# The RWKV-7 block's chunk inverses: 16 by 16 blocks by forward substitution on VectorE, then two doubling levels in place of five

## The reference, cut to what matters

```python
def wkv7_scan(r, decay, k, v, a_vec, b_vec):
    def step(s, inp):
        r_t, w_t, k_t, v_t, a_t, b_t = inp
        sa = jnp.einsum('bhvk,bhk->bhv', s, a_t)
        s = (s * w_t[:, :, None, :] + sa[..., None] * b_t[:, :, None, :]
             + v_t[..., None] * k_t[:, :, None, :])
        y = jnp.einsum('bhvk,bhk->bhv', s, r_t)
        return s, y
```

## Time and profile before

| | |
|---|---|
| median of 3 runs | 2805.22 us (2804.65 to 2805.6) |
| span of the profiled execution | 2808.4 us |
| TensorE busy, matmul / weight load | 2701.1 us (96%) / 2321.6 us (83%) |
| VectorE, ScalarE, GpSimd busy | 1584.7, 1051.3, 638.2 us |
| the chunk stage, from its first instruction to its barrier | 212.4 to 293.6 us |

### The profile page before, as it was taken

How to read it: one execution, slowest core, us unless ns; L and a number is a source line. 1 busy time by engine, 2 the same in 40 slices (tenths; PEclk the granted TensorE clock), 3 DMA queues, 4 the chain that set the end, 5 groups by cost and what they waited for, 6 DMA issues and landing times. The chain is left out here.

```text
span 2808.4 us, 42550 instructions
## 1 busy us (share of the span) xinstructions
PE 2701.1 (96%) x16610; PEld 2321.6 (83%) x16610; DVE 1584.7 (56%) x2463; ACT 1051.3 (37%) x1827; POOL 638.2 (23%) x518
## 2 busy tenths in 40 slices
PE   8999999999999999998999999999999999999998
PEld 6779877788888777877888888986888899999987
DVE  5976557466653456865533336975544446666643
ACT  4364333442222333354423224546443243322223
POOL 3430101221100113442100003346444320211101
PEclk9999899999999999999999999999899999999999
DMA  4200231122222322211322222210111132222221
GB/s 163 92 9 8 90 102 64 38 90 98 98 98 98 118 75 68 92 49 64 93 97 97 98 98 76 88 64 2 52 35 40 34 121 91 83 93 93 94 98 60
DMA packets 64276, 219.08 MB, mean 78 GB/s; under 512 B 8182, under 2 KB 8822, under 8 KB 63830
## 3 DMA queue, kind: packets, MB, share of 16 engines
q1 hardware_dynamic: 61190, 211.62, 22.6%
q10 hardware_dynamic: 2896, 4.82, 0.5%
HBM read 210.07 MB, written 6.32 MB: 77 GB/s over the span
## 5 line engine op out<-in xcount | busy, mean ns | idle before, releaser
L308 PE MATMUL ps<-normed,slab_parts 128*128 128x512 f32 (+3 forms) x2280 | 789.1, 346 | 24.8 <-DVE normed L650 11.2
L310 PE MATMUL ps<-normed,slab_parts 128*128 128x512 f32 (+3 forms) x2280 | 767.0, 336 | 0.0
L309 PE MATMUL ps<-normed,slab_parts 128*128 128x512 f32 (+3 forms) x2280 | 766.6, 336 | 0.0
L163 ACT ACTIVATE slab_parts<-ring 128x1024 fp32r<-128x1024 f32 x360 | 380.3, 1057 | 897.4 <-PE ps L310 879.9
L167 DVE TENSOR_TENSOR slab_parts<-ring,slab_parts 128x1024 fp32r<-128x1024 f32 x345 | 461.5, 1340 | 377.5 <-ACT slab_parts L163 374.6
L308 PEld LDWEIGHTS ps<-normed,slab_parts 128*128 128x128 f32 x2280 | 432.6, 190 | 79.6 <-issue 20.0
L309 PEld LDWEIGHTS ps<-normed,slab_parts 128*128 128x128 f32 x2280 | 432.7, 190 | 47.6 <-issue 5.3
L310 PEld LDWEIGHTS ps<-normed,slab_parts 128*128 128x128 f32 x2280 | 432.0, 189 | 44.5
L308 PE MATMUL ps<-hidden,slab_parts 128*128 128x512 f32 x560 | 219.2, 391 | 5.6 <-DVE hidden L258 5.6
L309 PE MATMUL ps<-hidden,slab_parts 128*128 128x512 f32 x560 | 219.0, 391 | 0.0
L310 PE MATMUL ps<-hidden,slab_parts 128*128 128x512 f32 x560 | 219.0, 391 | 0.0
(11 more groups left out here) (607 smaller groups left out, 4331.1 us busy)
## 6 DMA issues: line engine op xcount, KB each, us to landing
ring<-in_stream SPq DMA_DIRECT2D x376, 512.0 KB, 3.3
scratch_gates<-fox_y SPq DMA_DIRECT2D x12, 258.0 KB, 2.2
branch_gates<-scratch_gates ACTq DMA_DIRECT2D x1, 2064.0 KB, 15.1
h<-in_x SPq DMA_DIRECT2D x8, 256.0 KB, 6.2
scratch_fox_y<-fox_y SPq DMA_DIRECT2D x1, 1032.0 KB, 6.3
gdn_z<-scratch_gates ACTq DMA_DIRECT2D x1, 1032.0 KB, 4.9
fox_y<-scratch_fox_y ACTq DMA_DIRECT2D x1, 1032.0 KB, 17.2
mix_y<-in_sgu_b SPq DMA_DIRECT2D x1, 1024.0 KB, 6.5
```

The source lines that it names most:

```text
L163: self.nc.scalar.activation(self.hi[:, n % PARTS, :], self.ring[:, n % SLOTS, :], ACT.Copy).then_inc(self.hi_ready, 1)
L308: nc.tensor.matmul(to, lhsT[0], rhs[0], start=start, stop=False)
L309: nc.tensor.matmul(to, lhsT[0], rhs[1], start=False, stop=False)
L310: return nc.tensor.matmul(to, lhsT[1], rhs[0], start=False, stop=stop)
```

## The change

- The first part has four groups of products, not five: a by b, k by a, b by r, k by r. The group whose result was the transposed first level is gone.
- `LowerBlocks` is new. After VectorE has drained `amat` and `akT`, it turns the eight diagonal 32 by 32 squares of the 16 matrices (4 instructions, `take`), so that each of 128 partitions holds one 16 by 16 diagonal block; two instructions pick the right half. `solve` does forward substitution on all 128 blocks at once: 15 steps of a multiplication and an addition, each waiting for the one before. `place` writes the inverses back: two instructions and 4 transposes, into `invT`.
- Only the last two levels are left on TensorE (`LV = 2`), with the product by `amask` ahead of the transpose.
- The k by r result is copied out by ScalarE and masked by GpSimd; `amask` is made by GpSimd too. VectorE drains the b by r result after the inverses are placed.
- TensorE runs ten products of constants between the value products and the first level (`warm(K, 2, 10)`).
- The order of the block copies on ScalarE is b, a, r, no longer a, b, r. The mask transfer is two columns wider.

```diff
+BASE, SQUARE = 16, 32
+class LowerBlocks:
+    def windows(self, flat, g, n):
+        at = flat[g * SQUARE:(g + 1) * SQUARE, n * self.per * self.unit + g * SQUARE:]
+        return bass.AP(at.tensor, at.offset, [at.ap[0], [1, BASE], [BASE, 2], [self.unit, self.per]])
+    def turned(self, g, n):
+        return self.wide[g * SQUARE:(g + 1) * SQUARE, n].rearrange("p s (e u) -> p s e u", e=2)
...
+    def take(self, link):
+        for n in range(self.sets):
+            for g in range(self.groups):
+                last = nc.vector.transpose(self.turned(g, n), self.windows(self.amat, g, n))
...
+        link(last)
+        link(nc.vector.tensor_scalar(self.lower, self.wide[:, :, :, BASE:SQUARE], self.side(1, rows), None, ALU.mult))
+        link(nc.vector.scalar_tensor_tensor(out=self.lower, in0=self.wide[:, :, :, 0:BASE], scalar=self.side(0, rows), in1=self.lower, op0=ALU.mult, op1=ALU.add))
+    def solve(self, link):
+        for j in range(BASE - 1):
+            columns, rows = j + 1, BASE - 1 - j
+            product = self.part[:, :, 0:columns * rows].rearrange("p n (s r) -> p n s r", s=columns)
+            at = inverse[:, :, 0:columns, j + 1:BASE]
+            link(nc.vector.tensor_tensor(product, inverse[:, :, 0:columns, j:j + 1].to_broadcast((*shape, columns, rows)),
+                                         lower[:, :, j:j + 1, j + 1:BASE].to_broadcast((*shape, columns, rows)), ALU.mult))
+            link(nc.vector.tensor_tensor(at, at, product, ALU.add))
+    def place(self, link, placed):
+        for e in range(2):
+            link(nc.vector.tensor_scalar(self.wide[:, :, :, e * BASE:(e + 1) * BASE], self.inverse.rearrange("p n s r -> p n r s"), self.side(e, rows), None, ALU.mult))
+        for n in range(self.sets):
+            for g in range(self.groups):
+                last = nc.vector.transpose(self.windows(self.invT, g, n), self.turned(g, n))
+            last.then_inc(placed, 1)
...
-    PAIRS, LV = 2, LEVELS_R - 1
+    PAIRS, LV = 2, 2
...
+                pool.wait_ge(arrived, 16)
+                for q in range(PAIRS):
+                    pool.wait_ge(drained[q], 2)
+                    pool.wait_ge(filled[q], AMAT + 1)
+                    nc.gpsimd.tensor_tensor(amask[:, q], amat[:, q], level(0), ALU.mult).then_inc(masked[q], 1)
...
+                for q in range(PAIRS):
+                    for o in range(2):
+                        pool.wait_ge(rk_out, 2 * q + o + 1)
+                        nc.gpsimd.tensor_tensor(rk[:, 2 * q + o], rk[:, 2 * q + o], masks_in[CH:P, 2 * CH:3 * CH].unsqueeze(1).to_broadcast((CH, NCH, CH)), ALU.mult).then_inc(rk_masked, 1)
+                pool.wait_ge(rk_masked, 2 * PAIRS)
+                for q in range(PAIRS):
+                    pool.wait_ge(z_filled[q], 1)
+                    nc.gpsimd.tensor_tensor(amask[:, q], amat[:, q], level(1), ALU.mult).then_inc(masked[q], 1)
...
+                pe.wait_ge(w_out[0], 2)
+                warm(K, 2, 10)
+                pe.wait_ge(placed, 1)
                 for l in range(LV):
                     for q in range(PAIRS):
                         if l:
                             pe.wait_ge(d_added[q], l)
-                        for c in range(NCH):
-                            last = nc.tensor.transpose(two_banks(q, 2)[:, c, :], invT[:, q, c, :], K.ident)
-                        last.then_inc(turned[q], 1)
+                        else:
+                            pe.wait_ge(drained[q], 6)
                         pe.wait_ge(masked[q], l + 1)
```

More of the change, by code:

```diff
@@ L100, in shape_constants @@
     pair = [c[:, None] > c[None, :], c[:, None] < c[None, :], c[:, None] <= c[None, :], level(CH, 0).T]
[L101 removed]
+    sides = np.stack([i % 32 < 16, i % 32 >= 16], axis=1) * 1.0
+    lr = np.concatenate([np.tile(m, (2, 1)) for m in pair] + [np.kron(np.eye(2), level(CH, l)) for l in range(1, LEVELS_R)] + [sides], axis=1)
     lg = np.zeros((P, LEVELS_G + 5, C3))
@@ L1562, in _, with products @@
             @block.tensor
             def _(pe):
+                def products(q, b, tokens, heads):
+                    for c in range(NCH):
+                        last = nc.tensor.matmul(pair(q, b)[:, c, :], tokens[:, q, c * CH:(c + 1) * CH], heads[:, q, c, :], start=True, stop=True)
+                    last.then_inc(filled[q], 1)
                 warm(K, 0, 4)
[L1565 to L1569, removed]
-                        for c in range(NCH):
-                            last = nc.tensor.matmul(pair(q, n)[:, c, :], tokens[:, q, c * CH:(c + 1) * CH], heads[:, q, c, :], start=True, stop=True)
-                        last.then_inc(filled[q], 1)
@@ L1576, in _ @@
+                for q in range(PAIRS):
+                    pe.wait_ge(drained[q], 4)
+                    products(q, 2, k_t, r_blocks)
+                for q in range(PAIRS):
+                    pe.wait_ge(rk_out, 2 * q + 2)
                     for o in range(2):
@@ L1595, in _ @@
                         last.then_inc(z_filled[q], 1)
+                        if l:
+                            pe.wait_ge(inv_out[q], l)
+                        else:
+                            pe.wait_ge(w_out[q], 2)
+                        for c in range(NCH):
+                            last = nc.tensor.transpose(two_banks(q, 2)[:, c, :], invT[:, q, c, :], K.ident)
+                        last.then_inc(turned[q], 1)
                     for q in range(PAIRS):
@@ L1617, in _, with drain @@
                 link = Chain(dve, chain)
+                def drain(q, n, b, to):
+                    dve.wait_ge(filled[q], n + 1)
+                    for o in range(2):
+                        nc.vector.tensor_tensor(to(o), pair(q, b)[:, :, half[o]], mask((0, 1, 2)[n]), ALU.mult).then_inc(drained[q], 1)
                 nc.vector.memset(b_blocks[:], 0.0).then_inc(zeroed_too, 1)
@@ L1654, in _ @@
                             nc.scalar.activation(blocks(to, q, o), vectors(src, q, o), ACT.Copy).then_inc(ready, 1)
+                place(b_blocks, b_t, b_ready, zeroed_too, 1)
+                place(a_blocks, a_t, a_ready, zeroed, 1)
+                place(r_blocks, r_t, r_ready, zeroed, 2)
+                for q in range(PAIRS):
+                    act.wait_ge(filled[q], RK + 1)
+                    for o in range(2):
+                        nc.scalar.activation(rk[:, 2 * q + o], pair(q, 2)[:, :, half[o]], ACT.Copy).then_inc(rk_out, 1)
                 for q in range(PAIRS):
```

100 lines of the change are left out of this document (66 added, 34 removed).

## The result

| | before | changed |
|---|---|---|
| median | 2805.41 us (4 runs, 2804.65 to 2806.28) | 2788.55 us (4 runs, 2786.36 to 2788.99) |
| ratio, 95% interval | | 0.9935 [0.9921, 0.9949] |
| span of the profiled execution | 2808.4 us | 2785.0 us |
| GpSimd's first clearing to the last addition | 283.41 - 212.44 = 70.97 us | 265.67 - 211.83 = 53.84 us |
| the same, to ScalarE's first instruction of the next stage | 293.73 - 212.44 = 81.29 us | 275.99 - 211.83 = 64.16 us |

The kernel is 16.9 us faster by the medians; 17.7 was forecast, and the median of 2787.5 is 1.05 us under the measured one. The spans differ by 23.4 us.

The account below looks back on a forecast made before the run. The chunk stage's chain of waits bounds the kernel: first product at 247.8, plus 16.3 for two levels and 1.6 for the clock, puts the last addition at 265.7, 17.7 us earlier; median 2787.5 us, range 2780.5 to 2792.5.

Parts of the forecast that it names:

- What goes: Chunk stage: three levels of 8.89 us go, 26.7 us, and one product group of five; two levels left take 16.3.
- F: Start of the first level's first product on TensorE, forecast at 247.8 us in the trace.
- TensorE's own way to F: Chunk stage: four product groups, value products and ten products of constants have TensorE through at 242.7 us.
- VectorE's way to F: Chunk stage: drains, selections, substitution, eight transposes and the b by r drain end at 243.8 us, before GpSimd's holds.
- the port: Hold that GpSimd's masks put on VectorE's instructions during selections and substitution; 4.0 us, between 0 and 5.2.
- GpSimd's masks: Four k by r masks on GpSimd hold VectorE's two-input instructions 1.0 us each, 4.0 us in all.
- The clock: First level: TensorE idles 5 us before it, the granted clock falls, and the level takes 1.6 us more.
- A: Rival: GpSimd's masks hold VectorE little or not, F = 243.8 and the clock holds; 2781.9 us; chance 0.22.
- B: Rival: VectorE's transposes run at a copy's full rate, 3.4 us less, F = 244.4; 2784.1 us; chance 0.14.
- C: Rival: substitution, transposes or GpSimd's holds on VectorE are dearer, up to +6.1 us; 2793.6, middle 2791; chance 0.12.
- D: Rival: slower than before, transposes of 4.5 us each on VectorE, eight 27 us dearer; 2814.6 us; chance 0.03.
- E: Rival: three levels gone but something else in the chunk stage ends at the same time; no change seen, 0.02.

Follow-up runs that it names:

- e_const15: Changed kernel with fifteen products of constants ahead of the first level in place of ten; median 2786.50 us.
- e_nosolve: Changed kernel without the 30 instructions of the forward substitution, so its inverses are wrong; 2782.94 us (one run).
- e_contig: Changed kernel with the transposes' strided side made contiguous, same element count, so its inverses are wrong; 2789.45 us (one run).
- e_late_swap9: e_mask_late with the first level's product and transpose swapping banks, and nine products of constants for ten; median 2780.08 us.
- e_late_const0: e_mask_late without the ten products of constants; median 2783.02 us.
- e_side_without: The kernel of e_late_const0 measured again, side by side with the kernel of e_mask_late on the same chip; median 2787.08 us.
- e_const0: Changed kernel without the products of constants ahead of the first level; median 2789.49 us.
- e_mask_late: Changed kernel with GpSimd's four k by r masks moved behind its two masks for the last level; median 2783.02 us, ratio 0.9917 to before.

## Why the prediction was right

- **What goes.** The two levels left were to take 16.3 us from F at full clock. e_const15 has 51.55 - 35.28 = 16.27. The prediction's reading of the level as a fixed round of 8.89 us that no engine's share shortens stands: 8.89 to 9.00 in all kernels whose clock held. Right.
- **TensorE's own way to F**, 30.26 forecast, 30.32 in e_nosolve. Right.
- **VectorE's way to F**, 247.8 - 212.44 = 35.4 forecast, 35.20 measured. By terms: the substitution without the port 7.1 forecast; 240.50 - 230.29 = 10.21 less the 2.99 that three of its steps lost is 7.2. Its steps of 15 to 64 elements came as the row of one element and the slope of a copy said, not as the 0.28 of a two-tensor instruction of 64 elements. Transposes 1.1 forecast, 1.07 and 1.04 measured. The strided copy of 16 elements was the right neighbour in kind, since e_contig's 0.72 shows that the stride is what costs; that 15 ns of one row led to within 0.06 us of the measured length is partly luck. The drain of b by r was 1.3, and 1.34 by e_late_swap9. The selections were the one loose term: 1.65 forecast; 0.35, 0.48 (without the port) and 0.90 for the last two, with their waits 1.9. The turning began where the sum had it, 224.02 - 211.83 = 12.19 from the start for 224.6 - 212.44 = 12.16; the 0.2 us less are the eight transposes, 8.5 with their waits for 9.1, against small excesses in the other terms.
- **The Trainium skill's rule on strides.** The trace showed it: 1.04 to 1.07 us with a hop at every element, 0.72 without. The prediction's estimate of 1.0 to 1.4 us came from the 1.7 to 2.5 ns an element of the Trainium skill, Vector Engine (DVE) Microarchitecture Reference, section 5.2 "Measured stream behaviour on trn2"; its low end fits. It spoke against the change, and it was already in the sum.
- **GpSimd's masks.** Four holds of 1.0 us forecast, from the one row of 2.51 us; 4.04 measured, by taking them away. Right in place, number and size. The Trainium skill, SBUF — State Buffer, section "Who interferes with whom", says that an instruction of VectorE with two inputs in SBUF contends with one of GpSimd that reads SBUF. The rows agree as far as the two-tensor instructions go; e_nosolve has a case that this sentence does not cover (last section).
- **The clock: the step that was mis-sized.** I took the 1.6 us from the first level of the kernel before. It cost 2.38. The prediction read the price off one level and took it for a constant. By stretch, of the kernel before:

```profile
238.00:239.00 1.00, 0.14 (x2) 0.17 (x2) 1.00 (x2) 0.26 (x1) 0.00 (x0) 1.00 0.00 0
239.00:240.00 1.00, 1.00 (x6) 1.00 (x6) 0.74 (x1) 0.00 (x0) 0.00 (x0) 0.50 0.00 0
...
242.00:243.00 1.00, 1.00 (x9) 1.00 (x9) 0.00 (x0) 0.00 (x0) 0.00 (x0) 0.80 0.06 16
243.00:244.00 1.00, 1.00 (x12) 1.00 (x11) 0.61 (x1) 0.61 (x1) 0.00 (x0) 1.00 0.00 0
```

There the clock was at 0.50 from 239.0 to 242.4, so the level lost half of 3.4, 1.7 us. In the changed kernel it had fallen before the level began, and stood at 0.50 from the first product at 247.03 to 252.0: half of 4.9 is 2.5. The same reckoning fits the others: e_late_const0, 242.18 to 247.6, gives 2.7, and lost 2.61; e_side_without, 242.63 to 246.7, gives 2.0, and lost 1.96. So the price of a fallen clock is half the busy time spent at 0.50. Only 0.14 us of the difference between the two levels comes from the fall (0.14 us behind the first product in the kernel before, ahead of it in the changed one); the rest is that the clock came back 3.5 us after the first product in the one and 4.9 in the other. The length of the gap does not order these times: 4.9 behind gaps of 4.71 and 13.63 us (changed, e_const0), 5.4 and 4.1 behind 9.6 us (e_late_const0, e_side_without). What sets them is open. The term that was mis-sized is thus the 1.6 us, which measured 2.38; from one level it could only have been a range. That it would fall, and that ten products of constants would not prevent it, was right.
- **The sum.** F 0.2 us sooner, the levels 0.74 longer (18.64 for 17.9): the last addition at 53.84 from the start for 53.26, thus 17.1 us gained for 17.7. The prediction called itself wrong in the sum if the last additions did not begin 16 to 18 us after the first product. They begin 18.64 after it, outside by the clock's 0.64, while its other sign, a first product that waits for something else than VectorE, did not appear. F is closer than its terms, since the transposes' 0.6 us and the small excesses cancel in part; and that the medians give 16.9 for 17.1 is closer than they can be relied on, since each kernel's own runs spread by 1.6 and 2.6 us.
- **Rivals.** A needs the port not to hold VectorE and falls with the four long steps; e_mask_late is what A describes, but for 0.2 us, with 47.47 to the last addition for its 47.66. B, a transpose at the rate of a copy, falls with 1.07 and 1.04; e_contig shows what B would have been, and B itself left out that the clock would then have held. C and D fall with the steps of 0.18 to 0.23 and the same transposes. E falls with the stage's length. The gains of the edits do not add up one by one, since a shorter VectorE also closes TensorE's gap: 4.0 us of port are worth 6.4, 2.7 of stride are worth 5.0.

## What to carry to other kernels

When work leaves a chain of large instructions for a chain of small ones on another engine, sum the small chain by one row of one element plus a slope, then look which third engine reads the same memory meanwhile: moving GpSimd's four masks to where VectorE is idle was worth 6.4 us, more than a third of what the whole change brought. Constants that keep TensorE's clock up paid only where they reached nearly to the awaited product; count them from the gap (4.7 us here, 0.44 a record, two records a product, thus five more products), and recount them when the gap changes.

## What the runs showed of the hardware that I had not expected

- Behind the value products of 64 by 64, a gap of 1.23 us was followed by a fallen clock in the kernel before; behind products of constants of 128x512 gaps of 0.51, 0.72, 1.52 and 2.06 us left it at 1.00, and only that of 4.71 did not. What was busy before the gap differs between them, not only the gap's length; which of the two decides was not tried apart. Nor does one execution each show that the longer ones of these gaps always leave the clock alone: in e_late_const0 it was at 0.50 from 234.0 on, 1.4 us after TensorE's last record ended, while in e_side_without, the same kernel, it was still at 1.00 at 236.0, 3.0 us after.
- The same kernel had the clock back 5.4 us after its first product in one execution and 4.1 us after in another (e_late_const0, e_side_without), so the price of a fallen clock differs by 0.65 us in the same kernel (2.61 and 1.96).
- In e_nosolve two TENSOR_SCALARs with one tensor in SBUF and one factor for each partition took 2.71 us together beside GpSimd's masks, for 0.90 in the changed kernel, where GpSimd was idle. So instructions of VectorE with a single tensor from SBUF stood longer too, by 0.9 us each, and the masks are the one thing that ran beside them in the one kernel and not in the other; the run was not made to test this. The transposes, beside the last of these masks, kept their length (4.24 us, and 4.14 to 4.24 in the kernels whose masks were over by then). I had no row of the kernel before for such a case.
- In all of these GpSimd's masks took 4.95 to 5.42 us for four, whether VectorE stood beside them or not (4.98 in e_mask_late, where it had little to do): VectorE paid nearly all of the contention.
